# All 128-channel tiles of the mixers in three fp32r products, on one stream of 512 KB sheets shared with the dense layer

## What is computed

```python
h = rmsnorm(x, norm_mix)
za, zb, zc, zd, zg = split(h @ w_in)          # four mixers and their gates
ya = rwkv_mixer(za)                            # a recurrence, in chunks of 64 tokens
yb = dsa_attend(...)                           # attention over the 64 (72) best keys of an index score
yc = pool_mixer(zc)                            # moving averages
yd = swa(...)                                  # attention over a window, with sinks
m = sum_i sigmoid(zg[i]) * (y[i] @ w_branch[i])
x = x + m @ w_out
h = rmsnorm(x, norm_ffn)
layer 0: x = x + (silu(h @ f_gate) * (h @ f_up)) @ f_down      # 2816 hidden channels
layer 1: x = x + sum over the top 2 of 8 experts of the same form, 3584 hidden channels each
```

## Time and profile before

| | |
|---|---|
| median of 3 runs | 2113.63 us |
| the profiled execution | 2115.37 us, span 2113.5 us, mean clock 0.976 |
| TensorE busy | 2031.6 us (96%) |
| VectorE busy | 1420.0 us (67%) |
| ScalarE busy | 1023.4 us (48%) |
| GpSimd busy | 140.6 us (7%) |
| read from memory | 462.66 MB, 220 GB/s over the span |

### The profile page before, as it was taken

One profiled execution on the slowest core, in us unless ns is written; L12 is line 12 of the kernel. 1 busy time (PEld: TensorE's weight loads), 2 busy tenths in 40 slices (PEclk: granted clock), 3 DMA queues, 4 the chain that ended last, 5 costly groups with the idle time before them and its releaser, 6 DMA issues.

```text
span 2113.5 us, 27278 instructions
## 1 busy us (share of the span) xinstructions
PE 2031.6 (96%) x10340; PEld 1643.8 (78%) x10340; DVE 1420.0 (67%) x1750; ACT 1023.4 (48%) x1174; POOL 140.6 (7%) x108
## 2 busy tenths in 40 slices
PE   7999899989998999899989999999999999999998
PEld 5778566789997778666778787888878788787886
DVE  1453347277873443347278898988889888898987
ACT  1321243143331321134157676767677676776765
POOL 2000000154540000000000000000000000000000
PEclk9999999999999999899979999999999999999999
DMA  7321103324443321103349898999988999998995
GB/s 276 127 75 60 65 31 120 146 102 158 172 156 122 124 96 60 66 30 120 139 153 359 338 354 331 357 347 341 344 338 358 344 347 345 339 354 334 359 346 211
DMA packets 61577, 467.33 MB, mean 221 GB/s; under 512 B 7592, under 2 KB 7848, under 8 KB 9744
## 3 DMA queue, kind: packets, MB, share of 16 engines
q1 hardware_dynamic: 58896, 459.86, 57.7%
q0 software_dynamic: 2560, 5.85, 0.8%
HBM read 462.66 MB, written 3.02 MB: 220 GB/s over the span
## 4 chain that ended last, share of the span: by engine, by line
PE 92%; DVE 5%; ACT 2%; issue 1%; POOL 0%; DMA 0%; DVEq 0%; ACTq 0%; POOLq 0%
PE ps L504 13%; PE ps L961 10%; PE ps L966 10%; PE ps L963 10%; PE ps L651 8%; PE ps L986 5%; PE ps L992 5%; PE ps L987 5%; PE ps L672 3%; PE ps L852 2%; PE ps L856 2%; PE ps L859 2%; PE ps L930 1%; PE ps L974 1%; PE ps L875 1%; PE ps L876 1%
## 5 line engine op out<-in xcount | busy, mean ns | idle before, releaser
L1907 DVE TENSOR_TENSOR ring_r<-ring,unit_hi 128x2048 fp32r<-128x2048 f32 x288 | 652.9, 2290 | 111.0 <-ACT unit_hi L1383 108.5
L1383 ACT ACTIVATE unit_hi<-ring 128x2048 fp32r<-128x2048 f32 x288 | 542.7, 1913 | 0.0
L961 PE MATMUL ps<-unit_hi,hg_hi 128*128 128x512 f32 x896 | 251.2, 402 | 0.6 <-issue 0.6
L963 PE MATMUL ps<-unit_hi,hg_lo 128*128 128x512 f32 x896 | 241.8, 392 | 0.0
L651 PE MATMUL ps<-h,ring 128*128 128x288 f32 x768 | 222.1, 429 | 6.9 <-DVE arena L1595 5.2
L504 PE MATMUL ps<-h,ring 128*128 128x288 f32 x832 | 209.9, 415 | 9.7 <-DVE h L1499 9.7
L966 PE MATMUL ps<-ring_r,hg_hi 128*128 128x512 f32 x772 | 211.7, 396 | 0.0
L504 PEld LDWEIGHTS ps<-h,ring 128*128 128x128 f32 x832 | 161.5, 195 | 56.5 <-issue 11.5
L963 PEld LDWEIGHTS ps<-unit_hi,hg_lo 128*128 128x128 f32 x896 | 168.9, 189 | 37.2
L961 PEld LDWEIGHTS ps<-unit_hi,hg_hi 128*128 128x128 f32 x896 | 161.0, 189 | 35.6 <-issue 5.1
L651 PEld LDWEIGHTS ps<-h,ring 128*128 128x128 f32 x768 | 144.6, 199 | 48.2 <-DVE arena L1595 5.5
(11 more groups left out here) (385 smaller groups left out, 2819.5 us busy)
## 6 DMA issues: line engine op xcount, KB each, us to landing
ring<-in_w_exp SPq DMA_DIRECT2D x288, 1024.0 KB, 4.8
ring<-in_w_mix SPq DMA_DIRECT2D x44, 1536.0 KB, 6.7
unit<-in_w_exp SPq DMA_DIRECT2D x48, 1024.0 KB, 4.8
ring<-in_w_ffn SPq DMA_DIRECT2D x22, 1536.0 KB, 6.6
rel_table<-rel_row POOLq DMA_DIRECT2D x8, 256.0 KB, 9.1
const<-in_const SPq DMA_DIRECT2D x1, 1186.0 KB, 8.4
x<-in_xT SPq DMA_DIRECT2D x1, 1152.0 KB, 5.3
out_yT<-x SPq DMA_DIRECT2D x4, 288.0 KB, 2.2
```

The lines of the kernel that those rows point to most:

```text
L961: mm(out, hg_hi[:, hp, 4 * w + k, :], hi[:, 512 * k:512 * k + 512], start=(w == 0 and k == 0), stop=False)
L963: mm(out, hg_lo[:, hp, 4 * w + k, :], hi[:, 512 * k:512 * k + 512], start=False, stop=False)
L1383: fn(unit_hi(q), unit(q), ACT.Copy).then_inc(s["uhi_made"], 1)
L1907: v.tensor_tensor(unit_lo(q), unit(q), unit_hi(q).bitcast(F32), ALU.subtract).then_inc(s["ulo_made"], 1)
```

## The change

- All 58 tiles of a layer's mixers are multiplied in three fp32r products (`tile_part`), in the order weights hi x hi, hi x lo, lo x hi. The high part is copied by ScalarE into one of three places (`sheet_hi`), the low part is made by VectorE in place of the sheet (`sheet_lo`). Branch sheets stay fp32.
- h and m are split into `h_hi` (ScalarE) and `h_lo`, `m_lo` (VectorE).
- The ring is 8 slots of one sheet. Mixers and dense layer form one stream of 198 sheets, with one count `sheet_free`, raised at the first product of the next tile; the first units of the experts wait on it.
- ScalarE's copies (`high()`) stand behind the drain of each in tile, each gate's sigmoid, and so on; VectorE's subtractions (`low()`) stand in `time_shift`, `rwkv_vectors`, `qk_norm` (its reciprocal cut in three), `pooling`, behind each merge, and behind the adds of the out tiles.
- In the dense layer GpSimd does nothing any more; VectorE makes all three low parts of a step, and its order is new. The loops are written out.
- The relative table is flipped with 384 columns instead of 512. In a half of gates the order of the branch sheet and the first gate sheet is swapped.

```diff
-RING = 4
-MIX = 22
+MIX = 66
+FFN = 66
+RING = 8
+HIGHS = 3
-JW = 512
+JW = 384
@@ SyncE
-            for l in range(L):
-                for j in range(MIX):
...
+            for g in range(L * MIX + FFN):
+                if g == 3:
+                    sp.wait_ge(s["layer_in"], 16 * 12)
+                if g >= RING:
+                    sp.wait_ge(s["sheet_free"], g - RING + 1)
+                load(g)
...
-                            sp.wait_ge(s["chunk_free"], (1, 2, 2, 3, 4, 4)[q])
+                            sp.wait_ge(s["sheet_free"], (192, 194, 196, 198, 198, 198)[q])
@@ TensorE
+            def tile_part(out, hi, lo, i0, i1, free, hi_made=None, lo_made=None):
...
+                if i0 == 0:
+                    pe.wait_ge(s["hi_made"], c + 1)
+                for i in range(i0, i1):
+                    k = i % KD
...
+                    if i == 2 * KD - 1:
+                        pe.wait_ge(s["lo_made"], c + 1)
+                    ins = mm(out, (wl if i >= 2 * KD else wh)[:, k, :], (lo if KD <= i < 2 * KD else hi)[:, k],
+                             start=(i == 0), stop=(i == 3 * KD - 1))
...
+                    if i == 2 * KD - 1:
+                        ins.then_inc(s["hi_done"], 1)
@@ ScalarE
+            def high(count=1):
+                for _ in range(count):
+                    c = made[0]
+                    act.wait_ge(*sheet_in(SHEET_OF[c]))
+                    if c >= HIGHS:
+                        act.wait_ge(s["hi_done"], c - HIGHS + 1)
+                    fn(sheet_hi(c), sheet(SHEET_OF[c]), ACT.Copy).then_inc(s["hi_made"], 1)
+                    made[0] += 1
...
+                for c in range(C0):
+                    silu(c)
+                    high(min(3, FFN - 3 * c - 3))
@@ VectorE
+            def low(count=1):
+                for _ in range(count):
+                    c = made[0]
+                    dve.wait_ge(s["hi_made"], c + 1)
+                    v.tensor_tensor(sheet_lo(SHEET_OF[c]), sheet(SHEET_OF[c]), sheet_hi(c).bitcast(F32), ALU.subtract) \
+                        .then_inc(s["lo_made"], 1)
+                    made[0] += 1
+            def halves():
+                for k in range(KD):
+                    dve.wait_ge(s["h_hi_made"], n("h_hi_made"))
+                    v.tensor_tensor(h_lo[:, k], h[:, k], h_hi[:, k].bitcast(F32), ALU.subtract).then_inc(s["h_lo_made"], 1)
...
@@ VectorE, qk_norm
-                then(v.reciprocal(rstd, rstd))
+                for t in range(3):
+                    i = v.reciprocal(rstd[:, 2 * t:2 * t + 2], rstd[:, 2 * t:2 * t + 2])
+                    if t < 2:
+                        low()
@@ VectorE, merge
+                    if br != LAST:
+                        low()
@@ VectorE, dense
+                mult(0)
+                low(2)
+                for c in range(C0):
+                    if c < C0 - 1:
+                        mult(c + 1)
+                        low()
+                    add(c)
+                    low(min(2, FFN - 3 * c - 6) if c < C0 - 2 else 0)
@@ VectorE, the layers
+                low(HIGHS)
                 norm("norm_mix", 0)
+                halves()
+                low(6)
...
-                merge(l, LAST, 0, 8)
-                add_out()
+                for d in range(KD):
+                    merge(l, LAST, d, d + 1)
+                    if d:
+                        merged_halves(d - 1)
+                merged_halves(KD - 1)
+                low()
+                for d in range(KD):
+                    add_out(d)
+                    if d < 5 or l == 0:
+                        low()
```

More of the change, by code:

```diff
@@ L494, in norm_mean, with col_tile @@
                 i.then_inc(s["ms_full"], 1)
[L496 to L507, removed]
+            def col_tile(l, key, bank, signal, hi_made=None, lo_made=None):
+                tile_part(ps[:, bank, 0:T], h_hi, m_lo if key[0] == "out" else h_lo, 0, 3 * KD,
+                          (MIX + FFN) * l + SHEET_AT[key], hi_made, lo_made).then_inc(s[signal], 1)
             def in_tiles(l, t0, t1):
@@ L643, in gate_part @@
                 if k0 == 0:
-                    if d % 4 == 0:
-                        take(l, ("branch", br, d // 4))
-                    take(l, key)
                     if done:
                         pe.wait_ge(s["sig_made"], 24 * l + done)
-                w = sheet(l, key).rearrange("p (k c) -> p k c", k=KD)
-                for k in range(k0, k1):
-                    i = mm(ps[:, 0, 0:T], w[:, k, :], h[:, k], start=(k == 0), stop=(k == KD - 1))
-                    if k == 0:
-                        free_upto(i, l, SHEET_AT[key] - d % 4 - 1)
+                free = (MIX + FFN) * l + SHEET_AT[("gate", br, d - d % 4)] + (d % 4 > 0)
+                i = tile_part(ps[:, 0, 0:T], h_hi, h_lo, 3 * k0, 3 * k1, free) if k1 > k0 else None
                 if k1 == KD:
@@ L862, in gu @@
-                def gu(c, i):
-                    sheet_of("gate", c, i, 2 * (i % 2))
-                    sheet_of("up", c, i, 2 * (i % 2) + 1).then_inc(s["gu_full"], 1)
-                def down(c, i, static):
-                    r = room_of("down", i)
-                    pe.wait_ge(s["d_lo_made"], c + 1)
+                def gu(c):
+                    for q in range(2):
+                        first = c == 0 and q == 0
+                        i = tile_part(ps[:, 2 * (c % 2) + q, 0:T], h_hi, h_lo, 0, 3 * KD, SHEET_OF[tiles[0]],
+                                      ("h_hi_made", KD) if first else None, ("h_lo_made", KD) if first else None)
+                    i.then_inc(s["gu_full"], 1)
@@ L870, in down @@
+                def down(c):
+                    w = tiles[0]
+                    hi, lo = sheet_hi(w), sheet_lo(SHEET_OF[w])
+                    pe.wait_ge(s["hi_made"], w + 1)
+                    pe.wait_ge(s["lo_made"], w + 1)
                     pe.wait_ge(s["hT_made"], c + 1)
                     for d in range(KD):
-                        if not (static and 8 * c + d < 4):
+                        if 8 * c + d >= 4:
                             pe.wait_ge(s["ffn_added"], 8 * c + d - 3)
@@ L884, in dense @@
-                with pe.Fori(0, 4) as q:
-                    for i in range(RING):
-                        gu(4 * q + 4 + i, 4 + i)
-                        down(4 * q + 3 + i, 3 + i, False)
-                for c in (19, 20):
-                    gu(c + 1, c + 1)
-                    down(c, c, True)
-                down(21, 21, True)
+                        i = mm(out, hi[:, cols], hT_lo[:, c % 2], start=True, stop=False)
+                        if d == 0:
+                            free_before(i, SHEET_OF[w])
@@ L893, in experts @@
+                        i = mm(out, hi[:, cols], hT_hi[:, c % 2], start=False, stop=False)
+                        if d == KD - 1:
+                            i.then_inc(s["hi_done"], 1)
+                        mm(out, lo[:, cols], hT_hi[:, c % 2], start=False, stop=True).then_inc(s["down_full"], 1)
+                    tiles[0] += 1
+                gu(0)
+                for c in range(C0 - 1):
+                    gu(c + 1)
+                    down(c)
+                down(C0 - 1)
             def experts():
```

325 lines of the change are left out of this document (145 added, 180 removed).

## The result

The changed kernel takes 2164.76 us (median of 4 runs, 2161.99 to 2168.65), the kernel before 2114.38 us on the same chip; the ratio is 1.0241, with a 95% interval of 1.0223 to 1.0259. The forecast was 2150 us, slower. The profiled execution has a span of 2163.6 us and a mean clock of 0.953 (2113.5 and 0.976 before). In the later series one of 13 executions of the kernel before took 4063 us and one of 9 of the kernel with GpSimd 4852 us; both are slow ones and are left out of the comparisons.

A forecast was written before the change was run, and what follows sets the result against it. TensorE was taken as the bound, with nine tenths of the chain of waits. Mixers -9.5, dense layer +36.5 and clock +10 sum to +37 us; added to the median 2113.63 this gives 2150 us, range 2112 to 2182.

The forecast's parts named there:

- Dense stall: Dense layer: VectorE's first add comes late, so TensorE waits for PSUM banks; 2.13 us a step, 21 steps, 44.7 us lost.
- Given back: Dense layer: smoother start gains 3.9 us; last step, without stall or half clock, gains some 4.3 us.
- Clock: Dense steps: stalls may lower the granted clock, costing 0 to 36 us; 10 us taken.
- Input stage: Input tiles up to the recurrence: cheaper products partly lost to waits; 4.5 us gained in layer 0, 5.9 in layer 1.
- Attention: Attention: D steps gain 1.5 us, two full B steps lose 3.3 and 3.5; 4.6 us lost a layer.
- Flipped table: Layer 0's flipped relative table, 384 columns instead of 512: 1.5 us gained.
- Last merges and last step: Last branch merges, paced by VectorE, lose 2.8 us; the last attention step gives 0.7 us back.
- Out tiles: Output tiles of a layer: eight tiles save 0.70 us each, 5.5 us gained, nothing in the way.
- Recurrence: Recurrence with head norm: 0.7 us gained a layer; bounds 5.6 gained and 9.7 lost.
- the experts: Experts' stage: same instructions, first units loaded later but 30 us ahead of use; change of 0.
- Rival 1: Dense layer: the clock falls in every step; +63 us instead of +37, 2177 us; chance 0.14.
- Rival 2: Mixers, input and attention stages: added work hides, most of 81 us arrives; all of it gives 2070 us; chance 0.13.

The follow-up runs named there:

- the kernel with GpSimd: Adds first plus needless products in the recurrence's third block, with five low parts a layer moved from VectorE to GpSimd: 2108.35 us, against 2109.05 without the move.
- (c): Last branch's eight merges put before the low parts of m, one of three reorderings in a kernel of 2099.07 us; the same kernel without it took 2094.79 us.
- adds first: Changed kernel with VectorE making a dense step's eight adds before its low parts and multiplication, same instructions: 2118.93 us, ratio 1.0017 to the kernel before.

## Why the prediction was right in the main, and where not

The sign, the place and the mechanism were right. By its own terms:

- *Dense stall.* Forecast 2.13 us in 21 steps; measured 2.00 a step (11.58 - 9.58), 42 us. The silu ended where forecast (+0.60), the low part at +3.07 for +3.25, because VectorE's instructions overlap a little.
- *Given back.* The start: 3.9 forecast, 2.8 measured (first down product 28.8 us behind the norm's first product before, 25.9 after). The last step: 4.3 forecast, 4.7 measured (from its predecessor's first down product to the norm 11.1 us before, now 8.4 with that predecessor's stall of 2.0 in it). It does not stall and keeps its clock, as I had it.
- *Clock.* 10 us, a guess inside 0 to 36, came out as 12 us in the dense layer, 8 falls of 1.5 us. How many steps would fall no row told, so that this term came out near is luck. The dense sum is 42 - 2.8 - 4.7 + 12 = 46.5 measured, 44.7 - 3.9 - 4.3 + 10 = 46.5 forecast: the terms are off by 0.4 to 2.7 us, and cancel.
- *Input stage.* Start 4.1 us late: 4.2. Last gate tile: the low part was forecast for 127.8 and wanted at 123, a wait of 4.8; it began at 129.00, TensorE had come to it at 127.3 and waited 2.9. Saved up to the recurrence: 4.5 forecast and 2.6 measured in layer 0, 5.9 and 3.1 in layer 1 (norm included). Here too a part is clock, which the prediction priced only in the dense layer: from the lora products to the recurrence it was 1.00 in both layers before and 0.94 and 0.93 after.
- *Attention.* B steps +3.3 and +3.5: +3.5 and +2.3 us (17.9 to 21.4, 19.2 to 21.5 between turns). D steps -1.5: -2.0 up to the first B turn. *Flipped table* -1.5: -1.7 (10.5 to 8.8 us up to the first logits). *Last merges and last step*, +2.8 and -0.7, came out at +2.6, but the mechanism was wrong in part, as (c) shows: TensorE and VectorE pace each other. *Out tiles* -5.5: 31.28 to 25.77.
- *Recurrence.* This is the step that failed, -0.7 a layer. It is +1.4 in layer 0 and +9.0 in layer 1. The +1.4 is not the products' doing, for plain fp32 on the new stream has it too (116.1 and 116.0 us, before 114.7); the granted clock is 0.99 over this stage before and 0.97 there. In layer 1 the clock falls for 27 us in the third block. It did so in none of the three fp32 profiles, and without that fall three products take 116.0 us and fp32 115.9: they save nothing there, and the fall costs 8.9. I had priced clock only where a stall of 2 us stood and not where many short products follow each other. The two layers make 11.8 us of the 13 between the forecast's +37 and the +50 measured; the input stage adds 4.7, the stages from the head norm to the out tiles came out 3.9 better than forecast, the experts 0.5 worse.

Of 81 us of cheaper products the mixers got 5.9 us, less 9.0 in layer 1's recurrence. Rival 1 (every step's clock falls) is out: 8 of 21. Rival 2 is out: the input stage did not shrink to 95 us but to 108 (24.35 to 132.59). By the four passes of true fp32 (the Trainium skill, FP8 and Floating Point Precision, TensorE Precision Notes) three products would take three quarters of the time, an estimate of 23.5 us for out tiles of 31.28; they took 25.77.

## What to carry to other kernels

When work is added to an engine, count not its load but what now stands in front of the instruction that frees a buffer: VectorE was idle for 3.96 us of a step and still made TensorE wait 2 us, and moving the same instructions gave back 46 us. A cheaper matmul is worth its saving only where TensorE waits for nothing else, as in the out tiles (5.5 of 5.6 us) and hardly in stages paced by others. And shortening TensorE's filler work in a chain of small products can cost more clock than the products save (8.9 us in one block here), so look at the granted clock of each stretch before and after.

## What was not expected of the hardware

- 14 needless products in each of 21 stalls took seven of eight falls of the clock away and 10.5 us with them, and three behind each fill but a tile's last, in one short block of each layer, made the kernel 10 us faster.
- The same program can have the clock at half for 27 us in layer 1's third block and not in layer 0's (after), and the next kernel, the same up to there, in both layers: 8.7 to 9.0 us each time. The runs of adds first spread over 8.0 us (2113.89 to 2121.89), about one such fall; that it makes the spread is not shown.
- A VectorE instruction of four numbers a partition waits out a whole GpSimd subtraction (2.27 for 0.17 us), while in another of these overlaps (342.15 to 344.5) VectorE's searches for maxima kept their 0.43 us.
